# Another source for a 32 by 32 inverse, and other addresses in SBUF, in a three-block transformer kernel on Trainium2

## Time and profile before

| what | value |
|---|---|
| median of three runs | 3833.81 us (3827.45 to 3835.82) |
| profiled execution, its time | 3835.82 us |
| its span in the trace | 3834.0 us |
| TensorE / VectorE / ScalarE / GpSimd busy | 90% / 56% / 47% / 25% |
| first stretch of `rwkv_scan` | 3188.7 to 3271.6 us, 82.9 us |
| rest of `rwkv_scan` | 3271.6 to about 3350 us |

### The profile page before, as it was taken

The page is one execution under the profiler, slowest core; times in us unless marked ns, Lnnn a source line. Parts: engine busy times, 40 slices in busy tenths (PEclk is TensorE's granted clock), DMA queues, the critical chain, the costliest instruction groups (busy, mean ns, idle before and its releaser), DMA issues. The chain is left out here.

```text
span 3834.0 us, 56046 instructions
## 1 busy us (share of the span) xinstructions
PE 3464.3 (90%) x20889; PEld 2775.1 (72%) x20889; DVE 2149.0 (56%) x2889; ACT 1785.8 (47%) x2297; POOL 975.5 (25%) x435
## 2 busy tenths in 40 slices
PE   6989999869999999999999697899998886779997
PEld 4877777547777777777777483678877755658876
DVE  3310211359999999999999326511241263255665
ACT  3222333237787777777777434322342242133333
POOL 2334233201212222121212230134442300024443
PEclk9999999969999999999999898899998966789999
DMA  8223433249999999999999427123232200012221
GB/s 271 74 66 104 127 121 110 77 160 365 356 366 361 358 365 361 367 352 374 353 371 355 151 94 269 34 77 99 94 98 62 92 4 5 7 45 96 91 88 50
DMA packets 245432, 696.84 MB, mean 182 GB/s; under 512 B 17846, under 2 KB 149802, under 8 KB 186652
## 3 DMA queue, kind: packets, MB, share of 16 engines
q1 hardware_dynamic: 234956, 657.73, 46.6%
q0 software_dynamic: 9936, 36.18, 3.8%
q10 hardware_dynamic: 384, 0.65, 0.1%
HBM read 668.73 MB, written 30.23 MB: 182 GB/s over the span
## 5 line engine op out<-in xcount | busy, mean ns | idle before, releaser
L311 POOL TENSOR_TENSOR split_w<-ring,split_w 128x1024 fp32r<-128x1024 f32 (+1 forms) x294 | 700.2, 2382 | 1748.2 <-ACT split_w L306 1600.7
L1808 DVE TENSOR_TENSOR moe_low<-ring,moe_high 128x1024 fp32r<-128x1024 f32 x816 | 961.7, 1217 | 4.4 <-ACT moe_high L1800 4.2
L1800 ACT ACTIVATE moe_high<-ring 128x1024 fp32r<-128x1024 f32 x810 | 808.5, 1058 | 49.8 <-PE psum L2053 49.5
L306 ACT ACTIVATE split_w<-ring 128x1024 fp32r<-128x1024 f32 (+1 forms) x294 | 304.6, 1036 | 1020.5 <-PE psum L376 652.4
L2049 PE MATMUL psum<-moe_high,moe_xe 128*128 128x512 f32 x2176 | 586.6, 391 | 0.0
L2049 PEld LDWEIGHTS psum<-moe_high,moe_xe 128*128 128x128 f32 x2176 | 409.8, 188 | 85.5
L1962 POOL DMA_INDIRECT moe_y_rows<-moe_ye,moe_target x34 | 202.0, 5942 | 761.7 <-DVE moe_ye L1863 761.7
L376 PE MATMUL psum<-pair,split_w 128*128 128x512 f32 x1584 | 365.8, 394 | 11.2 <-PEq L128 4.7
L376 PEld LDWEIGHTS psum<-pair,split_w 128*128 128x128 f32 x1584 | 301.4, 191 | 74.8 <-issue 7.2
L376 PE MATMUL psum<-b_pair,split_w 128*128 128x512 f32 x1440 | 335.7, 395 | 14.5 <-PEq L838 8.8
L2053 PE MATMUL psum<-moe_low,moe_xe 128*128 128x512 f32 x1088 | 336.6, 391 | 0.0
(11 more groups left out here) (589 smaller groups left out, 4343.0 us busy)
## 6 DMA issues: line engine op xcount, KB each, us to landing
ring<-in_w_experts SPq DMA_DIRECT2D x408, 1024.0 KB, 6.5
ring<-in_w_mod SPq DMA_DIRECT2D x48, 1024.0 KB, 6.7
ring<-in_w_in SPq DMA_DIRECT2D x39, 1024.0 KB, 5.2
ring<-in_w_up SPq DMA_DIRECT2D x33, 1024.0 KB, 5.1
ring<-in_w_in SPq DMA_DIRECT2D x44, 512.0 KB, 5.2
ring<-in_w_down SPq DMA_DIRECT2D x20, 1024.0 KB, 5.0
ring<-in_w_gate SPq DMA_DIRECT2D x11, 1024.0 KB, 5.3
ring<-in_w_out SPq DMA_DIRECT2D x8, 1024.0 KB, 6.2
```

The lines of the kernel that those rows point to most:

```text
L306: self.nc.scalar.activation(high, raw, ACT.Copy).then_inc(self.K.rounded, 1)
L311: self.nc.gpsimd.tensor_tensor(low, raw, high.bitcast(F32), ALU.subtract).then_inc(self.K.split, 1)
L1800: self.nc.scalar.activation(self.B["high"][:, j % HALVES, :], self.raw(j), ACT.Copy).then_inc(self.high, 1)
L1808: self.nc.vector.tensor_tensor(self.B["low"][:, j % HALVES, :], self.raw(j), self.B["high"][:, j % HALVES, :].bitcast(F32), ALU.subtract). ...
```

## The change

Two things are done. First, all gaps go, and with them the placing of `b1_T0`, `b1_T12`, `b3_cols` and `b3_mods` on the right side: they are allocated on the left in the order of the code, so that many tiles of all three blocks start at other addresses. Second, `rwkv_scan` no longer transposes TT into T. TensorE makes alpha beta^T in the other orientation too (128 more calls into banks 6 and 7), VectorE makes the first T from it (one product with a mask, one subtraction), and at each of the first three levels TensorE also makes the product of TT and X (64 more calls a half, into banks 2 and 3), which VectorE subtracts from T. The semaphore `turned` goes; `aa_done` and `t_read` come.

```diff
-    def gap(self, ctx, name, nbytes, side="left"):
-        ctx.enter_context(self.nc.sbuf_tensor(f"{name}_gap", [P, nbytes // 4], F32, side=side))
...
-OWN_GAP = {"w_o": 64, "b2_out": 352, "b3_out": 256}
...
-                K.gap(ctx, f"{stage}_a", OWN_GAP[stage])
...
-                K.gap(mid, "b1_pair", 128)
-                pair = K.sb(mid, "b1_pair", [P, 2, KD, S], F32R)
-                T0 = mid.enter_context(nc.sbuf_tensor("b1_T0", [P, AH, T0W], F32, side="right"))
-                T12 = mid.enter_context(nc.sbuf_tensor("b1_T12", [P, AH, T12W], F32, side="right"))
...
+                T0, T12 = K.sb(mid, "b1_T0", [P, AH, T0W]), K.sb(mid, "b1_T12", [P, AH, T12W])
...
-        right = lambda name, shape: ctx.enter_context(K.nc.sbuf_tensor(f"b3_{name}", shape, F32, side="right"))
...
+        self.mods = K.sb(ctx, "b3_mods", [P, 4, KD])
...
-                K.gap(heads, "b2_pair", 32)
...
-        K.gap(K.pair_ctx, "pair", 320, "right")
...
+                for t in range(NT):
+                    ins = over_chunks(t, lambda c, cc, m, q: nc.tensor.matmul(
+                        ps[rows(cc), 6 + m, (t * 4 + c) * C:(t * 4 + c + 1) * C], alpha[half(m), c, q],
+                        beta[half(m), c, q], start=True, stop=True))
+                ins.then_inc(aa_done, 1)
...
                 both(0, beta).then_inc(ba_done, 1)
+                pe.wait_ge(t_read, 1)
                 both(4, kappa).then_inc(ka_done, 1)
...
-                        pe.wait_ge(turned, 2 * l + m if l else 1)
+                        pe.wait_ge(t_new, 2 * l + m if l else 1)
...
+                            if l < L - 1:
+                                for cc in range(CT):
+                                    ins = nc.tensor.matmul(ps[rows(cc), 2 + m, b * C:(b + 1) * C],
+                                                           TT[rows(cc), 16 * m + b, :], X[rows(cc), 16 * m + b, :],
+                                                           start=True, stop=True)
...
+                ve.wait_ge(aa_done, 1)
+                nc.vector.tensor_tensor(T, by(6, 2, C), mask(0), ALU.mult).then_inc(t_read, 1)
+                ve.wait_ge(t_read, 1)
+                nc.vector.tensor_tensor(T, ident, T, ALU.subtract)
...
-                ve.wait_ge(t_new, 1)
-                nc.vector.transpose(T.rearrange("p b n -> p (b n)"), TT.rearrange("p b n -> p (b n)")).then_inc(turned, 1)
...
+                        if l < L - 1:
+                            K.dve_link(nc.vector.tensor_tensor(T[:, hs, :], T[:, hs, :], by(2 + m, 1, C), ALU.subtract))
...
-                        if l < L - 1:
-                            nc.vector.transpose(T[:, hs, :].rearrange("p b n -> p (b n)"),
-                                                TT[:, hs, :].rearrange("p b n -> p (b n)")).then_inc(turned, 1)
```

More of the change, by code:

```diff
@@ L594, with __init__ @@
 class Columns:
-    def __init__(self, K, name, vectors, ctx, cols=None):
+    def __init__(self, K, name, vectors, ctx):
         self.K, self.vectors, self.at, r = K, vectors, {}, 0
@@ L603, in __init__ @@
         self.n = r
-        self.cols = K.sb(ctx, name, [P, r]) if cols is None else cols
-        self.raw = K.sb(ctx, f"{name}_rows", [P, P])
+        self.cols, self.raw = K.sb(ctx, name, [P, r]), K.sb(ctx, f"{name}_rows", [P, P])
         self.loaded, self.turned, self.copied = (K.sem(f"{name}_{s}") for s in ("loaded", "turned", "copied"))
@@ L2269, in block1 @@
         with nc.sbuf_tensor("b1_merged", [P, KD, S], F32) as merged:
-            with ExitStack() as mid:
-                K.gap(mid, "b1_pair", 128)
-                pair = K.sb(mid, "b1_pair", [P, 2, KD, S], F32R)
-                T0 = mid.enter_context(nc.sbuf_tensor("b1_T0", [P, AH, T0W], F32, side="right"))
-                T12 = mid.enter_context(nc.sbuf_tensor("b1_T12", [P, AH, T12W], F32, side="right"))
+            with nc.sbuf_tensor("b1_pair", [P, 2, KD, S], F32R) as pair, ExitStack() as mid:
                 with ExitStack() as entry:
@@ L2942, in __init__ @@
         vectors += [("ln_w", A["rwkv_ln_w_3"][0]), ("ln_b", A["rwkv_ln_b_3"][0]), *mod_bias(A["b_mod_3"][0])]
-        right = lambda name, shape: ctx.enter_context(K.nc.sbuf_tensor(f"b3_{name}", shape, F32, side="right"))
-        cols = right("cols", [P, sum(v.shape[0] for _, v in vectors) // P])
-        self.cols = Columns(K, "b3_cols", vectors, ctx, cols)
+        self.cols = Columns(K, "b3_cols", vectors, ctx)
         self.gates = K.sb(ctx, "b3_gates", [P, 2, D])
-        self.mods = right("mods", [P, 4, KD])
+        self.mods = K.sb(ctx, "b3_mods", [P, 4, KD])
     def col(self, key, n):
@@ L2975, in block2 @@
                            lambda i: first3 + 2 * i, (6,), (7,))
-            with ExitStack() as heads:
-                K.gap(heads, "b2_pair", 32)
-                pair = K.sb(heads, "b2_pair", [P, 2, KD, S], F32R)
+            with nc.sbuf_tensor("b2_pair", [P, 2, KD, S], F32R) as pair:
                 with ExitStack() as entry:
@@ L3439, in rwkv_scan @@
     n_ = lambda s: K.sem(f"rs_{s}")
-    ba_done, ka_done, turned, ba_read, ka_read, t_new, off_ready, xd, x_ready, tx = (
-        n_(s) for s in "ba ka turned baread karead tnew off x xready tx".split())
+    ba_done, aa_done, ka_done, t_read, ba_read, ka_read, t_new, off_ready, xd, x_ready, tx = (
+        n_(s) for s in "ba aa ka tread baread karead tnew off x xready tx".split())
     filled, taken, ud, at_ready, un_ready, corr_done, rt_ready, g_done, g_ready, ch, s_ready, yd, y_ready = (
```

## The result

The changed kernel takes 3888.97 us (median of 4 runs, 3887.84 to 3893.28) against 3833.32 us (4 runs, 3827.45 to 3835.82) for the kernel before in the same session: a ratio of 1.0151 [1.0137, 1.0166], or 55.6 us. The prediction was 3863 us, with 3849 to 3880 as its range. The profiled execution took 3893.18 us.

The account below looks back on a forecast made before the run. It took the scan's first stretch as bound by the arrival of TensorE's instructions. 3835.8 us profiled plus 29.2 for 8 blocks, with VectorE, transposes and addresses at nothing, gave 3865.0, so 3863.0 for a median; range 3849 to 3880.

Parts of the forecast that it names:

- The bound of the scan and the price of a block: Scan's first stretch: bound by arrival of TensorE's instructions; 8 added blocks at 3.65 us cost 29.2 us.
- Rival (a): Scan: block fetches are hidden and only the added calls' execution counts, 15.4 us, 3849 us; chance 0.09.
- rival (c): Scan: added matmuls slip into TensorE's waits, dependence sets the chain, 5.5 us of transposes go, 3828 us; chance 0.03.
- rival (d): Scan: nothing changes, the extra code is absorbed behind a later wait; chance 0.02.
- The 4 us estimated from the Trainium skill: Scan: added matmuls overlapping on different sub-arrays, about 4 ns of issue each, would cost some 4 us.
- VectorE's balance at nothing: Scan: 5.5 us of transposes go, 6.6 us of new operations come; the +1.1 us was costed at nothing.
- The transposes give nothing back: Scan levels: removing the transposes shortens no chain, since TensorE's instructions arrive later than their results; nothing given back.
- I cost the addresses at nothing: 512-column products on moved tiles: 4,080 products keep 226.7 ns between starts, as the experts' do; cost nothing.
- rival (b): Moved tiles: addresses matter because split_w and its partner no longer agree, up to 27 us more, 3890 us; chance 0.14.
- Its upper bound, 27 us: Moved tiles: most the addresses could cost, 6.6 ns x 4,080 products = 27 us.
- The 6.6 ns: Experts' stage: slowest group, six products in 1.40 us or 233.3 ns, against 226.7 ns.
- The count: 4,080 matmuls reading pair, b3_hpair and b3_out_a: 1584 + 720 + 1056 + 528 and half of 384.

Follow-up runs that it names:

- e2: Only the change's edits inside rwkv_scan, on the kernel before with its addresses kept: 3862.75 us, 1.0080.
- e5: Kernel before plus 512 one-column fp32 calls in the scan, results unread, VectorE's work and transposes kept: 3865.10 us, 1.0084.
- e6: Kernel before plus 256 unread one-column fp32 calls: 128 ahead of the first products, 128 in the first level: 3850.13 us, 1.0048.
- e7: Kernel before without the six transposes at the levels' ends, later levels using an old T: 3833.46 us, 1.0002.
- e1: Only the change's addresses (gaps gone, tiles moved to the left), with the scan of the kernel before: 3861.10 us, 1.0074.
- e3: Kernel before with split_w and all tiles behind it moved up 32 bytes together, differences still 0: 3831.92 us, 0.9996.
- e4: Kernel before with the tile pair alone moved up 32 bytes, split_w left in place: 3843.97 us, 1.0028.
- e10: Kernel before with other gaps (320, 224, 160, 96, 96, 192), so partner tiles lie at other distances from split_w; run once: 3856.11 us.

## Why the prediction was wrong, by its own steps

**The bound of the scan and the price of a block: right.** The step "one block of 256 in 3.65 us" gave 29.2 us. After has 29.4, e2 29.2 (112.07 - 82.90), e5 29.7, and e6 half of it. The Trainium skill, Runtime: NRT & Kernel Launch, section Instruction fetch mechanics, has a crossing mostly hidden behind the present block's execution. With 1-column calls the execution is shorter still, and e5 costs the same as e2; the trace disagrees with that rule for these bursts. Rival (a), only the execution, and rival (c), a stage set by its dependences, are out by the same runs; (c) also by e7. So is rival (d): e2's whole time grew by some 28 us, so nothing behind the stretch absorbed it. The 4 us estimated from the Trainium skill, TensorE: Matmul & The Clock Gate, Part 3, stand against 29.7 us in e5. Even within a burst that pace is not seen: the 92 one-column products in 1.02 us start some 9 ns apart.

**VectorE's balance at nothing: right.** Busy time in the stretch went from 23.25 to 24.85 us, and e2 is no slower than e5, in which VectorE does none of the new work. **The transposes give nothing back: right** (e7, 0.6 us at most in the stretch).

**"I cost the addresses at nothing": the step that failed.** It measured 26.1 us (e1). The row that it leaned on, 226.7 ns in the experts' stage with tiles at 32 modulo 64, is true, but both operands of those products start at 96, so d is 0; it answered whether the place matters (it does not, e3) and was used for whether the difference does. The prediction said that this very pairing had no row, gave it as rival (b) with 0.14, and cut the range at half of it. Rival (b) is what happened in kind. That the time, 3889.0 us, came within 1 us of its 3890 is luck, as the next point shows.

**Its upper bound, 27 us, was nearly right by luck.** The 6.6 ns came from a group of six products at 233.3 ns in the earlier trace rows, whose operands agree. That group (from 1000.36 us) follows products of another kind. In most stages of before, up to nine products after such a change stand 224 to 236 ns apart, about 232 in the mean, so that row showed the start of a run and not an address. That the mismatch costs the same 6.7 ns is a coincidence as far as these runs tell. The count was off as well. The 1,440 products of block 1 on `b1_pair` (d = 128, 232.4 ns), 192 on `b1_retpair` (233.3), 192 on `w_o_a` and 192 on `b2_out_a` were left out, and 192 of the 720 on `pair` have 256 columns and lose nothing (117 to 120 ns with any d). Counted with the measured spacing, the moving side is 1,440 x 5.7 + 192 x 6.6 + 1,584 x 6.6 + 1,056 x 6.6 = 26.9 us and the stationary side 528 x 7.5 + 528 x 6.5 + 384 x 5 + 192 x 2.3 = 9.8 us, 36.7 in all. The measured 26.1 is less because part of it is taken back in waits: 2.0 us ahead of the experts, and 2.2 us where L518 waits for `b_hpair` (9.7 us, 11.9 before). About 6 us of what is taken back I have not placed; e4 shows the same, 14 us by count and 9 to 11 measured. The scatter is as large as that: by its interval the 26.1 us of e1 are 22 to 35, and one burst ahead of the scan (L239, 64 small products) took 12.8 us in before's trace and 10.4 in that of e7, where nothing was changed that far up.

## What to carry to other kernels

Where TensorE is the bound, place the moving and the stationary tile of 512-column fp32r products at the same remainder modulo 256 bytes; 96, 128 and 160 modulo 512 did equally well here. Look at the spacing of the products, not at the busy share. When a row stands in for a case that has none, write down in which property the two differ before you price the gap at nothing, and then let the bound of the unknown into the range. In a stage of small fp32 calls, count instructions first: there the price was 3.7 us for each 256, whatever they computed.

## What the runs showed of the hardware that was not expected

A 512-column fp32r product takes 226.7 ns from start to start when its operands start at the same remainder modulo 256 bytes. For most other distances it takes 6.6 to 6.7 ns more, which is 16 cycles at the 2.4 GHz that is granted in these stages (0.99 of full speed from 2509 to 2740 us, before and after), and at most 7.6 ns more. A distance of 64 costs only 2.2 ns, though in two of the groups it cost 6.7. It is the same whether `split_w` moves or stands still (e4: 233.3 ns on either side).

Products of 256 columns get no slower (113 to 120 ns at the full clock), and some get faster. Timeline of TensorE on `b2_pair` in before (d = 0), then in e10 (d = 192):

```profile
2269.83 13.48 PE L362 MATMUL psum<-split_w,b_pair 128*128 128x256 f32 x111
```

```profile
2269.77 9.80 PE L362 MATMUL psum<-split_w,b_pair 128*128 128x256 f32 x85
```

Less 0.28 us for the last product, that is 13.20 / 110 = 120.0 ns and 9.52 / 84 = 113.3. What that is worth in time was not tried by itself. Why any of this is so, no run here shows.
